# Key transposes one projection block earlier, and eight products in place of 32 behind the key products

## The chip, the cores and the metric

The kernel runs on one core of a Trainium2 chip. The metric is the device time of one execution in microseconds, the median of several. Nothing of the computation runs on the host, which only lays the arrays out.

## The reference

Three layers work on 256 tokens of width 1024 (and on 256 context tokens in the first): a hybrid mixer (gated delta rule beside attention) with a feed-forward part, a convolution layer with another, and a third layer of three branches. All is float32. The change lies in the gated delta rule of the first layer. Cut to that:

```python
decay = exp(where(incl, gcum[:, None] - gcum[None, :], -inf))
kb = kc * bc                                   # keys times beta
lower = where(strict, kb @ kc.T * decay, 0.0)  # one matrix for each chunk, head and direction
sol = triangular_solve(lower + eye, rhs, unit_diagonal=True)
```

The keys `kc` come from a projection, a convolution of five taps over the tokens, silu and a normalisation to length one. The rule runs once forward and once backward over the tokens, for 4 heads of width 128.

## The kernel before

The program is written out by hand for each engine: TensorE (PE), VectorE (DVE), ScalarE (ACT), GpSimd (POOL) and SyncE, which issues the weight loads. Each engine works through its own list in the order of the code, and semaphores tie the lists together; no scheduler moves anything. PSUM has eight banks, each given out in turns: `wait_full` waits until TensorE has filled a bank, `freed` gives it back.

The first layer's projection has twelve blocks of 128 features, numbered 0 to 11 (0 to 3 keys, 4 to 7 values, 8 to 11 queries). Blocks 0 to 4 are multiplied from weights that are split in two parts, a high one that ScalarE rounds (`part_high`, L1704) and a low one that VectorE subtracts (`part_low`, L2259); TensorE takes both in L987. The later blocks are multiplied in full precision (L789). ScalarE moves each block out of PSUM (`features_evac`, L1653), VectorE convolves it (`conv5`, L2306 and L2310) and ScalarE applies silu (`conv_silu`, L1659).

When key blocks 0 to 3 are through silu, TensorE turns them to rows of tokens (`to_tok`, L743), ScalarE squares and copies them (L1675, L1676), VectorE sums the squares (L2318) and scales the rows to length one (`unit_rows`, L2332). TensorE turns the scaled keys back (`to_feat`, L743 again), ScalarE copies (`to_features`, L1683), and TensorE multiplies the keys with each other, four products of one bank each (`kk`, L1026), one for each of the four stretches of 128 tokens. TensorE does projection blocks 5 and 9 between `to_tok` and `to_feat`, block 10 ahead of `kk`, and 11, 8, 6 and 7 behind it.

Each bank of key products then gives two matrices, one for each direction, in `U_t`: products times beta times decay, L2349. Beta differs by row and head, so each matrix takes four instructions of 128x128, one a head: 32 in all. The decays were written by ScalarE long before (`decays`, L1667); for stretches 0 and 1 they stand in `decay`, for 2 and 3 in `U_t` itself.

VectorE then transposes 32x32 blocks (L2359) beside ScalarE, which copies the other direction's blocks (L1762) when all four `ut_ready` are there and it has moved block 8 out of PSUM. From both VectorE builds the inverse of 32x32 blocks: L2362, 31 steps of L2368 and L2369, then L2396 and L2397. TensorE's products L1137 need the last of these. The wide part of the delta rule, the attention and the modulation products (L772, whose weights are loaded at that time) follow. Meanwhile, from 82.7 us to 112.1 us, GpSimd rotates and scales the attention's queries and keys (L2830 to L2855).

Of the kernel before, what the change touches and what calls it, by code (L numbers as in the profile page):

```python
# [25 lines left out]
ALU = mybir.AluOpType  # L26
# [4 lines left out]
P = 128  # L31
D = 1024
# [5 lines left out]
NH = 4  # L38
# [144 lines left out]
USE = {}  # L183
# [167 lines left out]
def build(nc, w, w_mod1, cols_in, rows_in, consts_in, b_out_in, c_bd_in, glu_in, b_in, x_in, ctx_in, out):  # L351
    ctx = ExitStack()
    w = {**w, "mod1": w_mod1}
    with ctx:
# [22 lines left out]
        def bc_in(ap, n):  # L377

            return ap.unsqueeze(2).to_broadcast([ap.shape[0], ap.shape[1], n])
# [18 lines left out]
        arena, arena_r = sb_both("arena", 16384)  # L398
        tok_t = sb("tok", TT * (HYB_T - 512) + TT * CTX_T)
        z_t, z_r = sb_both("z", TT * 512)  # L400
        o_t, o_r = sb_both("o", 1024)
# [26 lines left out]
        def bank(use):  # L428
            b = use[0] if isinstance(use, tuple) else use
            return psum[:, 512 * b:512 * b + 512]  # L430
# [51 lines left out]

        a_hi = [view(x, at, 2, 2 * T) for x, at in ((ybuf_r, 0), (ybuf_r, D), (arena_r, 2 * D), (arena_r, 3 * D))]
        a_lo = [view(x, at, 2, 2 * T) for x, at in ((yT_r, 0), (yT_r, D), (rowbc_r, 0), (diag_r, 0))]
        part_hi = [arena_r[:, 6144:6144 + D], o_r[:, 0:D], arena_r[:, 14432:14432 + D]]
        cv = view(arena, 0, 12, 2, T)
        cin = view(arena, 8192, 12, 2, T + 4)
        zgate = view(z_t, 0, TT, 512)
# [14 lines left out]
        U_t = [arena[:, 6144 + 512 * n:6656 + 512 * n] for n in range(4)] + [nrm_t[:, 512 * n:512 * n + 512] for n in range(4)]  # L503
        U_of = [view(arena, 6144, 16, P), view(nrm_t, 0, 16, P)]
        decay = view(decay_t, 0, 4, 512)
# [24 lines left out]
        beta = beta_t.rearrange("p (s e) -> p s e", s=4)  # L530
# [59 lines left out]
        kq_tok, kq_scaled, ut_ready, blocks_copied = sem("kq_tok"), sem("kq_scaled"), sem("ut_ready"), sem("blocks_copied")  # L590
# [78 lines left out]
        def wait_read(eng, use):  # L669
            eng.wait_ge(bank_free[use[0]], use[1] + 1)  # L670
# [4 lines left out]
        def freed(ins, use):  # L675
            ins.then_inc(bank_free[use[0]], 1)
# [56 lines left out]
        def _(pe):  # L733
# [268 lines left out]
            def hyb_features(c, blocks):  # L1002
                wait_ring(CHUNK["hyb_f", c])
                for b in blocks:
                    use = USE["hyb_f"][b]
                    wait_free(pe, use)
                    width = 2 * T if b < 8 else T
                    filled(feature_block(use, slot(CHUNK["hyb_f", c])[:, (b % 3) * D:(b % 3 + 1) * D],
                                         lambda k: aT[:, k, 0:width]), use)
# [27 lines left out]
            use = USE["gates"]  # L1037
# [15 lines left out]
                seq, t = (n // 2, n % 2)  # L1053
                transposes(USE["to_tok"][n], [cv[:, hh, seq, t * P:(t + 1) * P] for hh in range(NH)])
            hyb_features(1, (5,))
            hyb_features(3, (9,))
            for n in range(4):
                pe.wait_ge(kq_scaled, n + 1)
                transposes(USE["to_feat"][n], [ktok[:, n, hh * P:(hh + 1) * P] for hh in range(NH)])
            hyb_features(3, (10,))  # L1060
            for n in range(4):
                wait_read(pe, USE["to_feat"][n])
            for st in range(4):
                use = USE["kk"][st]
                wait_free(pe, use)
                kk = lambda hh: feat(kT[:, st // 2], st, hh)
                filled(per_head(use, kk, kk), use)
            hyb_features(3, (11,))
            hyb_features(2, (8, 6, 7))
            hyb_tokens(0)  # L1070

# [59 lines left out]
            for d in range(2):  # L1131
                use = USE["p5"][d]
                wait_free(pe, use)
                x, xt = inverse_of(d)
                for m in range(16):
                    for src, dst in PAIRS[d]:
                        last = mm(bank(use)[rows_of_block(dst), BLK * m:BLK * (m + 1)],  # L1137
                                  U_of[d][rows_of_block(src), m, rows_of_block(dst)], x[rows_of_block(src), m, :],
                                  start=True, stop=True)
                filled(last, use)  # L1140
            pause("p5")
            for d in range(2):
                wait_read(pe, USE["p5"][d])
                use = USE["q5"][d]
                wait_free(pe, use)
                x, xt = inverse_of(d)
                for m in range(16):
                    p = blk_p[:, 16 * d + m, :]
                    for src, dst in PAIRS[d]:
                        mm(bank(use)[rows_of_block(src), BLK * m:BLK * (m + 1)], p[rows_of_block(dst)],  # L1150
                           xt[rows_of_block(dst), m, :], start=True, stop=True)
                    src, dst = PAIRS[d][d]
                    last = mm(bank(use)[rows_of_block(dst), BLK * m:BLK * (m + 1)], xt[rows_of_block(dst), m, :],
                              p[rows_of_block(dst)], start=True, stop=True)
# [6 lines left out]
            for half, use in enumerate(USE["p6"]):  # L1161
                wait_free(pe, use)
                for m in range(8 * half, 8 * half + 8):
                    for d in range(2):
                        last = mm(bank(use)[halves[1 - d], 64 * (m % 8):64 * (m % 8 + 1)], U_of[d][halves[d], m, halves[1 - d]],
                                  X2[halves[d], m, :], start=True, stop=True)
# [8 lines left out]
            for half, use in enumerate(USE["q6"]):  # L1175
                wait_read(pe, USE["p6"][half])
                wait_free(pe, use)
                for m in range(8 * half, 8 * half + 8):
                    for d in range(2):
                        last = mm(bank(use)[halves[d], 64 * (m % 8):64 * (m % 8 + 1)], blk_p2[halves[1 - d], m, :],  # L1180
                                  XT_m[halves[1 - d], 16 * d + m, halves[1 - d]], start=True, stop=True)
# [25 lines left out]
            for s in range(4):  # L1207
                for d in range(2):
                    st = ORDER[d][s]
                    if s:  # L1210
                        wait_read(pe, USE["ds", s - 1, d])
                        use = USE["ks", s, d]
# [7 lines left out]
                for d in range(2):  # L1220
                    st = ORDER[d][s]
# [4 lines left out]
                    use = USE["vn", s, d]  # L1226
# [3 lines left out]
                if s >= 2:  # L1230
                    for d in range(2):
                        st = ORDER[d][s]
                        use = USE["os", s, d]
# [4 lines left out]
                if s < 3:  # L1238
                    for d in range(2):
                        wait_read(pe, USE["vn", s, d])  # L1240
                        pe.wait_ge(ktail_ready, 2 * s + d + 1)
                        use = USE["ds", s, d]
# [5 lines left out]
                if s >= 2:  # L1248
                    for d in range(2):
                        wait_read(pe, USE["vn", s, d])  # L1250
                        use = USE["oi", s, d]
# [68 lines left out]
            for n, src in enumerate((cc, csq)):  # L1320
                use = USE["ln"][n]
                wait_free(pe, use)
                order = [*CONV_PE, *(k for k in range(KT) if k not in CONV_PE)] if n == 0 else range(KT)
                for i, k in enumerate(order):
# [4 lines left out]
                    last = mm(bank(use)[:, 0:T], ones, src[:, k, :], start=(i == 0), stop=(i == KT - 1))  # L1329
# [83 lines left out]
            for i in range(S5T):  # L1413
# [7 lines left out]
                if i == 10:  # L1421
                    pe.wait_ge(logf_ready, 1)
                    use = USE["cum"]
# [19 lines left out]
            for n in range(NPAIR + 2):  # L1443
                if n < NPAIR:
                    pair, t = n // 2, n % 2
                    use = USE["fa_s"][n]
# [3 lines left out]
                    for half in range(2):  # L1450
                        q = slice(64 * half, 64 * half + 64)
                        last = mm(fa_scores[:, half, 0:(t + 1) * P], q2T[q, pair, t * P:(t + 1) * P], k2T[q, pair, 0:(t + 1) * P],  # L1452
                                  start=True, stop=True)
                    filled(last, use)
                    next(filler, None)
                if n >= 3 and n % 2:
                    pair = (n - 3) // 2
                    use = USE["fa_o"][pair]
                    wait_read(pe, USE["fa_t"][2 * pair + 1])
                    wait_free(pe, use)  # L1460
                    for kb, t0 in ((0, 0), (1, P)):
                        for half in range(2):
                            q0, at = 64 * half, (2 * pair + half) * AHD
                            last = mm(bank(use)[q0:q0 + 64, t0:T], v2[:, kb, at:at + AHD], fa_pT[pair % 2][:, half, kb, t0:T],
                                      start=(kb == 0), stop=(kb == 1))
# [16 lines left out]
            for j in range(8):  # L1482
# [3 lines left out]
                at = (j % 2) * 12 * P  # L1486
                for part in range(2):
                    use = USE["branch"][2 * j + part]
                    wait_free(pe, use)
                    for br in ((0, 1), (2,))[part]:  # L1490
                        for k in range(4):
                            wat = at + (4 * br + k) * P
                            last = mm(bank(use)[:, (br % 2) * T:(br % 2 + 1) * T], slot(c)[:, wat:wat + P],  # L1493
                                      ys[br][:, k, :], start=(k == 0), stop=(k == 3))
# [8 lines left out]
        def _(act):  # L1503
            fn = nc.scalar.activation
            ch = Chain(act, act_c)
# [142 lines left out]
            def features_evac(blocks):  # L1648
                for b in blocks:
                    use = USE["hyb_f"][b]  # L1650
                    wait_full(act, use)
                    n = 2 if b < 8 else 1
                    freed(fn(cin[:, b, 0:n, 2:T + 2], bank(use)[:, 0:n * T].rearrange("p (s t) -> p s t", s=n), ACT.Copy), use)  # L1653
# [75 lines left out]
            use = USE["gates"]  # L1729
# [22 lines left out]
            to_tokens(range(4))  # L1752
            act.wait_ge(kq_ms, 1)
            fn(kq_ss[:, 0:16], kq_ss[:, 0:16], ACT.Sqrt).then_inc(kq_sd, 1)
            features_evac((5, 9))
            to_features(range(4))
            features_evac((10,))
            conv_silu(5, (4,))
            features_evac((11, 8))
            act.wait_ge(ut_ready, 4)  # L1760
# [75 lines left out]
            for b in range(4):  # L1836
                last = fn(XT_m[rows_of_block(b), 0:16, rows_of_block(b)], xt[rows_of_block(b)], ACT.Copy)
# [5 lines left out]
            use = USE["q5"][0]  # L1843
# [3 lines left out]
            for src, dst in PAIRS[0]:  # L1847
                last = fn(XT_m[rows_of_block(src), 0:16, rows_of_block(dst)], grid[rows_of_block(src)], ACT.Copy, scale=-1.0)
# [5 lines left out]
            use = USE["q5"][1]  # L1854
# [212 lines left out]
        def _(dve):  # L2067
# [188 lines left out]
            def part_low(n):  # L2256
                dve.wait_ge(hyb_hi, 4 + n + 1)
                width = HYB_PARTS[n][3]
                tt(part_of(n, ring_r), part_of(n, ring), part_hi[n % 3][:, 0:width].bitcast(F32), ALU.subtract).then_inc(hyb_lo, 1)  # L2259
# [42 lines left out]
            def conv5(blocks):  # L2302
                n = 2 if blocks[0] < 8 else 1
                for b in blocks:
                    wait_read(dve, USE["hyb_f"][b])
                    ch.mark(ts(cv[:, b, 0:n, :], cin[:, b, 0:n, 0:T], taps[:, b, 0:1], None, ALU.mult))  # L2306
                for k in range(1, CONV_A):
                    ch.sync()
                    for b in blocks:
                        last = stt(cv[:, b, 0:n, :], cin[:, b, 0:n, k:k + T], taps[:, b, k:k + 1], cv[:, b, 0:n, :], ALU.mult, ALU.add)  # L2310
                        if k < CONV_A - 1:
                            ch.mark(last)
                last.then_inc(conv_done, 1)
# [18 lines left out]
                    tt(quad(x), quad(x), bc_in(kq_r[:, 4 * n:4 * n + 4], P), ALU.mult).then_inc(kq_scaled, 1)  # L2332

            conv5((0,))
            part_low(10)
            for b in range(1, 5):
                conv5((b,))
            unit_sums(0, 4)
            unit_rows(0, 4, None)
            conv5((5,))  # L2340
            for st, use in enumerate(USE["kk"]):
                wait_full(dve, use)
                for d in range(2):
                    n = 4 * d + st
                    wait_read(dve, USE["decay"][n])
                    src = decay[:, 2 * d + st, :] if st < 2 else U_t[n]
                    for hh in range(NH):
                        at = slice(hh * P, (hh + 1) * P)
                        last = stt(U_t[n][:, at], bank(use)[:, at], beta[:, st, 4 * d + hh:4 * d + hh + 1], src[:, at], ALU.mult, ALU.mult)  # L2349
                        if (d, hh) == (0, NH - 1):  # L2350
                            last.then_inc(ut_ready, 1)
                        elif hh == NH - 1:
                            freed(last, use)


            for use in USE["kk"]:
# [686 lines left out]
```

## Time and profile before

| | us |
|---|---|
| time, median of 3 runs (1362.14 to 1367.49) | 1363.67 |
| the profiled execution | 1363.14 |
| its span | 1361.1 |
| TensorE busy | 1279.1 (94%) |
| VectorE busy | 869.8 (64%) |
| ScalarE busy | 509.7 (37%) |
| GpSimd busy | 124.5 (9%) |

The page counts an engine as busy while an instruction stands on it, also if that instruction waits inside for something that no semaphore shows. The stretch that the change touches lies between 97 and 185 us of the span. All times below are counted from the span's start.

### The profile page before, as it was taken

Reading aid. Unit: us, or ns where it says so; the run is one execution under the profiler, and the core shown is the slowest. Engines: PE = TensorE matmul, PEld = TensorE weight load, DVE = VectorE, ACT = ScalarE, POOL = GpSimd, SP = SyncE. Lnnn points to the kernel's source line nnn. Section 1 sums busy time; section 2 is a strip of 40 time slices with the busy share of each in tenths; the row PEclk is TensorE's granted clock in tenths of the full one; section 3 lists DMA queues with packets and bytes.
Section 4 is the critical chain, followed back from the end, with each engine's and each line's share of the span. In section 5 each row is a group of like instructions: output and inputs, shape, how many; then the busy total and the mean of one; then the engine's idle time right before and its main releaser. Section 6 shows DMA issues by size and latency. Waiting matters only on the chain. (4 is left out here: it accounts for less than half of the span.)

```text
span 1361.1 us, 18882 instructions
## 1 busy us (share of the span) xinstructions
PE 1279.1 (94%) x7158; PEld 988.9 (73%) x7158; DVE 869.8 (64%) x1498; ACT 509.7 (37%) x850; POOL 124.5 (9%) x165
## 2 busy tenths in 40 slices
PE   3899979988999998999899999899999999899997
PEld 1687646553888887884588888777878885688886
DVE  1448796543876665795677777399962342777776
ACT  2474256323433444014544444312223321544443
POOL 0043022000000002000000000245520000000000
PEclk9899979999999999998899999899999999899999
DMA  9222367884555542421455555125233233455551
GB/s 391 89 112 77 138 269 287 356 353 180 195 189 186 185 155 70 155 94 47 185 186 185 185 185 198 66 78 185 93 139 127 106 109 123 155 185 185 185 189 58
DMA packets 24946, 225.75 MB, mean 166 GB/s; under 512 B 2737, under 2 KB 2865, under 8 KB 4658
## 3 DMA queue, kind: packets, MB, share of 16 engines
q1 hardware_dynamic: 23328, 220.31, 43.9%
q10 hardware_dynamic: 1554, 4.56, 0.9%
q8 instruction: 44, 0.72, 0.2%
q14 instruction: 20, 0.16, 0.0%
HBM read 223.81 MB, written 1.05 MB: 165 GB/s over the span
## 5 line engine op out<-in xcount | busy, mean ns | idle before, releaser
L872 PE MATMUL psum<-aT_r,arena_r 128*128 128x512 f32 x920 | 327.4, 398 | 1.4 <-DVE arena_r L2191 1.4
L2191 DVE TENSOR_TENSOR arena_r<-ring,arena_r 128x1024 fp32r<-128x1024 f32 x193 | 226.0, 1221 | 112.4 <-ACT arena_r L1599 112.4
L789 PE MATMUL psum<-aT,ring 128*128 128x256 f32 (+1 forms) x1136 | 266.3, 392 | 1.5 <-DVE aT L2148 1.5
L873 PE MATMUL psum<-aT_r,arena_r 128*128 128x256 f32 x920 | 258.2, 281 | 0.0
L789 PEld LDWEIGHTS psum<-aT,ring 128*128 128x128 f32 x1136 | 214.8, 191 | 47.9 <-issue 20.6
L1599 ACT ACTIVATE arena_r<-ring 128x1024 fp32r<-128x1024 f32 x193 | 191.5, 1050 | 149.6 <-PE psum L913 132.4
L913 PE MATMUL psum<-arena_r 128*128 128x512 f32 x876 | 213.5, 392 | 0.0
L872 PEld LDWEIGHTS psum<-aT_r,arena_r 128*128 128x128 f32 x920 | 172.8, 188 | 43.7 <-issue 1.9
L913 PEld LDWEIGHTS psum<-arena_r 128*128 128x128 f32 x876 | 159.5, 188 | 34.8
L873 PEld LDWEIGHTS psum<-aT_r,arena_r 128*128 128x128 f32 x920 | 173.7, 189 | 2.6
L1611 ACT ACTIVATE nrm<-nrm 128x256 f32<-128x256 f32 x76 | 31.8, 418 | 170.8 <-DVE nrm L2205 170.8
L772 PE MATMUL psum<-ring,cond 128*32 128x384 f32 x512 | 55.1, 560 | 20.2 <-DMA consts<-in_consts 12.4
L2205 DVE TENSOR_REDUCE nrm<-psum 128x256 f32<-128x512 f32 x76 | 51.9, 683 | 4.2 <-PE psum L883 4.2
L2535 DVE SCALAR_TENSOR_TENSOR arena<-arena,cols 128x256 f32<-128x256 f32 x120 | 52.8, 482 | 1.9
L772 PEld LDWEIGHTS psum<-ring,cond 128*32 128x32 f32 x512 | 15.2, 120 | 48.6 <-issue 36.0
L756 PE MATMUL psum<-consts,nrm 128*128 128x128 f32 x96 | 20.0, 382 | 29.5 <-DVE nrm L2121 27.5
L2219 DVE TENSOR_TENSOR nrm<-nrm 128x256 f32<-128x256 f32 x76 | 32.4, 426 | 21.8 <-ACT nrm L1611 16.1
L2209 DVE TENSOR_REDUCE nrm<-psum 128x256 f32<-128x512 f32 x44 | 30.4, 691 | 20.8 <-PE psum L873 20.8
L756 PEld LDWEIGHTS psum<-consts,nrm 128*128 128x128 f32 x96 | 16.5, 199 | 33.8 <-DVE nrm L2121 30.2
L2310 DVE SCALAR_TENSOR_TENSOR arena<-arena,cols 128x512 f32<-128x512 f32 (+1 forms) x48 | 35.3, 763 | 1.1
L1987 ACT ACTIVATE arena<-psum,cols 128x256 f32<-128x256 f32 x24 | 11.4, 474 | 58.2 <-PE psum L789 58.2
L2227 DVE TENSOR_TENSOR arena_r<-nrm,arena_r 128x256 fp32r<-128x256 f32 x73 | 31.1, 425 | 2.5
(495 smaller groups left out, 1642.3 us busy)
## 6 DMA issues: line engine op xcount, KB each, us to landing
ring<-in_w_ffn SPq DMA_DIRECT2D x44, 1536.0 KB, 6.5
ring<-in_w_mod SPq DMA_DIRECT2D x32, 1536.0 KB, 8.7
ring<-in_w_ff SPq DMA_DIRECT2D x32, 1024.0 KB, 4.9
ring<-in_w_in_g SPq DMA_DIRECT2D x8, 1536.0 KB, 6.4
ring<-in_w_conf_i SPq DMA_DIRECT2D x8, 1024.0 KB, 4.8
ring<-in_w_hyb_f SPq DMA_DIRECT2D x4, 1536.0 KB, 6.6
ring<-in_w_in_a SPq DMA_DIRECT2D x4, 1536.0 KB, 6.4
ring<-in_w_in_b SPq DMA_DIRECT2D x4, 1536.0 KB, 6.3
```

The costliest lines, as they stand in the source:

```text
L756: last = nc.tensor.transpose(bank(use)[:, j * T + t * P:j * T + (t + 1) * P], src[:, t, k * P:(k + 1) * P], ident)
L772: last = mm(mod_acc[q:q + 32, :], cond[:, at:at + 32], slot(c)[:, k * MOD_C:(k + 1) * MOD_C], start=(m == m0 and k < 4), stop=(m == m1 - 1 ...
L789: last = mm(bank(use)[:, out_at:out_at + rhs(k).shape[1]], weights[:, k * P:(k + 1) * P], rhs(k), start=(k == 0), stop=(k == KT - 1))
L872: mm(bank(use).rearrange("p (a t) -> p a t", a=2), hi, x_both[:, :, k, :], start=(k == 0), stop=False)
L873: last = mm(bank(use)[:, T:2 * T], lo, x_hi[:, k, :], start=False, stop=(k == KT - 1))
L913: last = mm(Y[:, t, half * 512:half * 512 + 512], act_part, w_part[:, half * 512:half * 512 + 512], start=(isinstance(i, int) and j == 0 a ...
L1599: fn(out_hi[2] if last_out else w_hi[j % 2][:, at], slot(c)[:, at], ACT.Copy).then_inc(split_hi, 1)
L2191: tt(lo, slot(c)[:, at], hi.bitcast(F32), ALU.subtract).then_inc(split_ready, 1)
L2205: summed = v.reduce_sum(g_sum[:, j % 2, :], bank(gate).rearrange("p (a t) -> p t a", a=2), axis=AXX)
L2219: tt(h_tmp, sg[:, j % 2, :], u_sum if parts == 3 else sg[:, j % 2, :], ALU.mult).then_inc(h_step, 1)
L2310: last = stt(cv[:, b, 0:n, :], cin[:, b, 0:n, k:k + T], taps[:, b, k:k + 1], cv[:, b, 0:n, :], ALU.mult, ALU.add)
L2535: last = stt(cc[:, c, :], cu[:, c, k:k + T], dww[:, c, k:k + 1], cc[:, c, :], ALU.mult, ALU.add)
```

## The change

VectorE multiplies the decays by beta ahead of the key products: eight instructions of 128x512, placed behind the convolution of block 0 and ahead of `part_low(10)`. Behind the key products stand eight instructions of 128x512 (`U_t` times a PSUM bank) in place of 32. TensorE does projection block 9 behind the `to_feat` transposes and not ahead of them, and block 10 behind `kk` and not ahead of it; ScalarE's copies follow suit. One buffer of rounded weights (`part_hi[0]`) moves, since `U_t` is now written while it is in use.

```diff
-        part_hi = [arena_r[:, 6144:6144 + D], o_r[:, 0:D], arena_r[:, 14432:14432 + D]]
+        part_hi = [arena_r[:, 4096:4096 + D], o_r[:, 0:D], arena_r[:, 14432:14432 + D]]
...
             hyb_features(1, (5,))
-            hyb_features(3, (9,))
             for n in range(4):
                 pe.wait_ge(kq_scaled, n + 1)
                 transposes(USE["to_feat"][n], [ktok[:, n, hh * P:(hh + 1) * P] for hh in range(NH)])
-            hyb_features(3, (10,))
+            hyb_features(3, (9,))
             for n in range(4):
                 wait_read(pe, USE["to_feat"][n])
...
                 filled(per_head(use, kk, kk), use)
-            hyb_features(3, (11,))
+            hyb_features(3, (10, 11))
             hyb_features(2, (8, 6, 7))
             hyb_tokens(0)
...
-            features_evac((5, 9))
+            features_evac((5,))
             to_features(range(4))
-            features_evac((10,))
+            features_evac((9, 10))
             conv_silu(5, (4,))
             features_evac((11, 8))
             act.wait_ge(ut_ready, 4)
...
             conv5((0,))
+            for n in range(8):
+                d, st = n // 4, n % 4
+                wait_read(dve, USE["decay"][n])
+                src = decay[:, 2 * d + st, :] if st < 2 else U_t[n]
+                ch.mark(tt(quad(U_t[n]), quad(src), bc_in(beta[:, st, 4 * d:4 * d + 4], P), ALU.mult))
             part_low(10)
             for b in range(1, 5):
                 conv5((b,))
             unit_sums(0, 4)
             unit_rows(0, 4, None)
             conv5((5,))
+            ch.sync()
             for st, use in enumerate(USE["kk"]):
                 wait_full(dve, use)
-                for d in range(2):
-                    n = 4 * d + st
-                    wait_read(dve, USE["decay"][n])
-                    src = decay[:, 2 * d + st, :] if st < 2 else U_t[n]
-                    for hh in range(NH):
-                        at = slice(hh * P, (hh + 1) * P)
-                        last = stt(U_t[n][:, at], bank(use)[:, at], beta[:, st, 4 * d + hh:4 * d + hh + 1], src[:, at], ALU.mult, ALU.mult)
-                        if (d, hh) == (0, NH - 1):
-                            last.then_inc(ut_ready, 1)
-                        elif hh == NH - 1:
-                            freed(last, use)
+                tt(U_t[st], bank(use), U_t[st], ALU.mult).then_inc(ut_ready, 1)
+                freed(tt(U_t[4 + st], bank(use), U_t[4 + st], ALU.mult), use)
```

VectorE's list of the changed kernel behind the convolution of block 0 (L2305 and L2309; in the kernel before they are L2306 and L2310): L2338 are the new products, L2258 is `part_low(10)`.

```order
L2309 SCALAR_TENSOR_TENSOR arena<-arena,cols 128x512 x4
L2338 TENSOR_TENSOR arena<-decay,small 128x512 x2
L2338 TENSOR_TENSOR arena<-arena,small 128x512 x2
L2338 TENSOR_TENSOR nrm<-decay,small 128x512 x2
L2338 TENSOR_TENSOR nrm<-nrm,small 128x512 x2
L2258 TENSOR_TENSOR ring_r<-ring,o_r 128x1024
```

In the kernel before `part_low(10)` stands right behind the convolution; eight instructions have moved in between, all of them ahead of the convolutions of blocks 1 to 4.

TensorE's list of the kernel before, from the `to_tok` transposes (the first L743) to the attention's; L789 are blocks 5 (128x512), then 9, the `to_feat` transposes, 10, the key products (L1026), 11 with 8, then 6 with 7:

```order
L743 MATMUL psum<-consts,arena 128x128 x16
L789 MATMUL psum<-aT,ring 128x512 x8
L789 MATMUL psum<-aT,ring 128x256 x8
L743 MATMUL psum<-consts,arena 128x128 x16
L789 MATMUL psum<-aT,ring 128x256 x8
L1026 MATMUL psum<-arena 128x128 x16
L789 MATMUL psum<-aT,ring 128x256 x16
L789 MATMUL psum<-aT,ring 128x512 x16
```

The same place in the changed kernel:

```order
L743 MATMUL psum<-consts,arena 128x128 x16
L789 MATMUL psum<-aT,ring 128x512 x8
L743 MATMUL psum<-consts,arena 128x128 x16
L789 MATMUL psum<-aT,ring 128x256 x8
L1026 MATMUL psum<-arena 128x128 x16
L789 MATMUL psum<-aT,ring 128x256 x24
L789 MATMUL psum<-aT,ring 128x512 x16
```

The second transposes and the key products each stand one block of eight 128x256 products earlier; what TensorE has done by the end of block 8 is the same set of instructions in both.

## Rows read from the trace of the kernel before

**Rows 1.** Timeline of VectorE: start, length, line, shapes, count, idle before and releaser

```profile
95.14 1.93 DVE L2259 TENSOR_TENSOR ring_r<-ring,arena_r 128x1024 fp32r<-128x1024 f32 x1 [4.05 <-ACT arena_r L1704]
...
97.69 6.03 DVE L2310 SCALAR_TENSOR_TENSOR arena<-arena,cols 128x512 f32<-128x512 f32 x4
107.61 1.23 DVE L2259 TENSOR_TENSOR ring_r<-ring,o_r 128x1024 fp32r<-128x1024 f32 x1 [3.88 <-ACT o_r L1704]
108.75 1.79 DVE L2306 TENSOR_SCALAR arena<-arena,cols 128x512 f32<-128x512 f32 x1
...
114.79 0.48 DVE L2306 TENSOR_SCALAR arena<-arena,cols 128x512 f32<-128x512 f32 x1
...
118.86 3.12 DVE L2310 SCALAR_TENSOR_TENSOR arena<-arena,cols 128x512 f32<-128x512 f32 x4
```

**Rows 2.** Timeline of GpSimd beside it

```profile
94.44 1.54 POOL L2843 TENSOR_TENSOR ring<-ring,rows 128x640 f32<-128x640 f32 x1
...
97.34 1.71 POOL L2843 TENSOR_TENSOR ring<-ring,rows 128x640 f32<-128x640 f32 x1
...
99.99 1.90 POOL L2848 TENSOR_TENSOR ring<-ring,consts 128x640 f32<-128x640 f32 x1
101.86 2.61 POOL L2851 TENSOR_TENSOR ring<-ring,consts 128x320 f32<-128x320 f32 x2
104.43 1.57 POOL L2848 TENSOR_TENSOR ring<-ring,consts 128x640 f32<-128x640 f32 x1
105.96 1.71 POOL L2851 TENSOR_TENSOR ring<-ring,consts 128x320 f32<-128x320 f32 x2
107.74 4.23 POOL L2855 TENSOR_TENSOR ring<-ring 128x640 f32<-128x640 f32 x2
```

**Rows 3.** Timeline of TensorE from the last product of block 4

```profile
122.09 0.39 PE L987 MATMUL psum<-arena_r,ring_r 128*128 128x512 f32 x1
122.69 1.53 PE L743 MATMUL psum<-consts,arena 128*128 128x128 f32 x12 [0.22 <-ACT arena L1659]
...
140.64 2.84 PE L1026 MATMUL psum<-arena 128*128 128x128 f32 x24
143.95 1.16 PE L1026 MATMUL psum<-arena 128*128 128x128 f32 x8 [0.47 <-DVE nrm L2349]
```

**Rows 4.** Timeline of ScalarE

```profile
122.01 0.63 ACT L1659 ACTIVATE arena<-arena 128x512 f32<-128x512 f32 x1 [2.92 <-DVE arena L2310]
...
152.05 0.39 ACT L1653 ACTIVATE arena<-psum 128x256 f32<-128x256 f32 x1 [3.07 <-PE psum L789]
152.33 2.57 ACT L1762 ACTIVATE yT<-arena 32x512 f32<-32x512 f32 x4
```

**Rows 5.** Timeline of VectorE from the scaled keys on

```profile
130.08 2.50 DVE L2332 TENSOR_TENSOR arena<-arena 128x512 f32<-128x512 f32 x4
...
141.73 1.12 DVE L2349 SCALAR_TENSOR_TENSOR arena<-psum,small,decay 128x128 f32<-128x128 f32 x4 [5.38 <-PE psum L1026]
...
150.23 2.90 DVE L2359 STREAM_TRANSPOSE yT<-nrm 32x512 f32<-32x512 f32 x4
...
155.00 2.09 DVE L2362 STREAM_TRANSPOSE diag<-yT 128x1024 f32<-128x1024 f32 x1 [1.87 <-ACT yT L1762]
```

**Rows 6.** Timeline of TensorE, its three waits that the clock is read beside

```profile
184.46 1.10 PE L1137 MATMUL psum<-yT,arena 32*32 32x32 f32 x58 [2.08 <-DVE yT L2397]
...
533.22 3.40 PE L756 MATMUL psum<-consts,nrm 128*128 128x128 f32 x16 [4.33 <-DVE nrm L2121]
...
862.98 3.67 PE L756 MATMUL psum<-consts,nrm 128*128 128x128 f32 x16 [4.25 <-DVE nrm L2121]
```

**Rows 7.** Windows: busy us by engine, then granted TensorE clock, DMA share, GB/s

```profile
186.00:188.00 2.00, 2.00 (x54) 1.48 (x53) 1.97 (x3) 1.87 (x4) 1.88 (x3) 0.50 0.98 418
...
534.00:536.00 2.00, 2.00 (x11) 1.72 (x10) 1.58 (x5) 0.14 (x1) 0.96 (x4) 0.50 0.00 0
...
868.00:870.00 2.00, 2.00 (x6) 1.64 (x5) 0.00 (x0) 0.00 (x0) 1.84 (x4) 0.50 0.00 0
```

## The prediction

> **What bounds the kernel now.** I read the page first (TensorE has work on it for 94% of the span), then the timelines of each engine from 95 to 185 us, then the waits there. I follow back what the changed stretch hands on. TensorE's products L1137 at 184.46 waited 2.08 us for VectorE's L2397 [rows 6]; that is the end of VectorE's inversion, which runs without a gap from L2362 at 155.00 on. L2362 itself sat idle for 1.87 us until ScalarE's copies L1762 had ended, although VectorE's own work of the key products was done by 153.13 (150.23 + 2.90) [rows 5]. L1762 came right behind ScalarE's move of block 8 at 152.05, for which ScalarE had waited 3.07 us on TensorE [rows 4]. So the chain is: TensorE's list up to the end of block 8, ScalarE's move and copies, VectorE's inversion, TensorE again. VectorE's 32 products L2349 are not on it: they end before L2362 could start, with 1.87 us to spare.
>
> TensorE's list up to block 8 has few gaps. Two matter. Ahead of the `to_tok` transposes it waits 0.22 us for silu of block 3, and inside the key products 0.47 us for a bank that L2349 held [rows 3]. Silu of block 3 starts at 122.01 [rows 4], right when VectorE's convolution of block 3 ends (118.86 + 3.12 = 121.98) [rows 1]. VectorE therefore has no slack at 122 us: it and TensorE arrive together. Its one free time before is the 3.88 us ahead of `part_low(10)` at 107.61 [rows 1].
>
> **The change part by part.**
>
> *Eight products in place of 32.* Before, VectorE takes 8.5 us from 141.73 to 150.23. After, eight products of 128x512; the nearest row is L2332, 2.50 us for four, 0.625 each, so about 5.0 us. With `kk` one block earlier they would end near 143.5 and the transposes near 146.5. Saved on VectorE's list: some 6 us. On the chain: nothing, since L2362 still waits for ScalarE's copies, which wait for block 8. What is late next is the same thing as now. The one gain is the 0.47 us of TensorE's bank wait: a bank is now freed 1.3 us after it is filled, and three further fills of 0.9 us come first.
>
> *The reordered blocks.* Up to the end of block 8 TensorE does the same instructions. The scaled keys come at 130.7 to 132.6 (four of L2332 from 130.08) and `to_feat` would start at 131.9, so the earlier transposes wait for at most a tenth or two. Block 9's weights are there already, block 10's bank too. Cost and gain: nothing.
>
> *The eight products ahead.* They are 8 x 0.625 = 5.0 us of VectorE's time, put ahead of `part_low(10)`, where 3.88 us are free. Were this all, `part_low(10)` would start at 103.72 + 5.0 = 108.7 instead of 107.61. But GpSimd is at work there until 111.97 [rows 2], and the rows show what that does. The TENSOR_SCALAR at 108.75 took 1.79 us against 0.48 at 114.79, while an L2855 ran, and the four SCALAR_TENSOR_TENSOR at 97.69 took 6.03 us against 3.12 at 118.86 [rows 1]. The TENSOR_TENSOR at 95.14, the kind that is added, took 1.93 us against 1.23 for the same shape at 107.61, under L2843 [rows 1, 2]. GpSimd's own two L2855 stretched as well. VectorE and GpSimd take turns there, an instruction at a time.
>
> From 103.72 on GpSimd still has 0.75 us of L2851, 1.57, 1.71, and two L2855 (4.23 us less the some 1.4 that they stood blocked): 6.9 us of its own work. How much of it VectorE loses has two bounds. The four instructions at 97.69 lost 2.9 us while GpSimd went through L2843, L2848, one L2851 and a small one between, about 4 us by their shorter rows (1.54, 1.57, 0.86) [rows 2]: 0.7 of it, which is 4.8 us here. Block 1's convolution, 108.75 to 114.79, took 6.04 us; blocks 2 and 3 together, 114.79 to 121.98, took 7.19, or 3.6 each [rows 1]. The two L2855 thus took 2.4 us from VectorE for 2.8 of their own, 0.9 of it: 6.2 us here. I take 5.2, nearer the first, as L2848 and L2851 are the same instructions. Block 1's convolution does not lose its 2.4 us again: it now comes after GpSimd is done.
>
> So VectorE: 103.72 + 5.0 (products) + 1.14 (`part_low`) + 5.2 (turns lost) = 115.1. TensorE needs `part_low(10)` for block 4, whose 24 products of 0.23 us begin about 5.5 us ahead of 122.3 [rows 3], at 116.8: 1.7 us of cover are left, and with the upper bound 0.7. Then three convolutions, 3 x 3.6 = 10.8: block 3 ends at 125.9 in place of 121.98. That is 3.9 us late (3.5 to 4.9), and nothing hides it: silu, `to_tok` and, in ScalarE's list, the move of block 4 and all of the key chain are behind it, and TensorE's list stands.
>
> **The sum.** +3.9 at `to_tok`, -0.5 at `kk`, all else moves along (the loads behind these blocks too, as they wait for their slots): +3.4 us. The profiled execution would go from 1363.14 to 1366.5; it lies 0.5 us under the median, so 1363.67 + 3.4 = 1367.1. A difference of under 0.5% (6.8 us) is about what a measurement of this kernel cannot tell from none.
>
> The Trainium skill ("SBUF — State Buffer", section Who interferes with whom) says that a VectorE instruction with two SBUF inputs and a GpSimd instruction that reads SBUF exclude each other for the whole instruction. By that rule alone, with no overlap at the handovers, the loss would be the full 6.9 us and the total +5.1; the rows show 0.7 to 0.9 of it, so I go by them.
>
> **The rivals.**
>
> *TensorE's clock falls in the new gap, for short.* TensorE would sit idle from 122.5 to about 126.6, 4.1 us. After idle times of 4.33 and 4.25 us the granted clock read 0.50, the lower of its two levels, and after 2.08 us with light work around it too [rows 6, 7]. Against it: dense work comes right before and behind. At half clock half of the time is lost: some 3.4 us low costs 1.7, total +5.1, 1368.8. Chance 25%.
>
> *The same, for long: slower by over 0.5%.* From 862 to 870 us the clock stayed low [rows 7]. The change is slower by over 0.5% if the clock is low for more than (6.8 - 3.4) / 0.5 = 6.8 us of work in blocks 5, 9 and the key products. With 10 us it would be +8.4, 1372.1. For it: that row. Against it: there work was thin until 867, here it is not. Chance 13%.
>
> *The products ahead are hidden.* If the new form, whose second input is a small broadcast, is not held up by GpSimd, `part_low(10)` ends at 109.9, block 1's convolution meets only the last L2855 (1.2 us lost), the three end at about 121.9, and only the 0.5 us at `kk` remains: 1363.2. For it: no row shows this form beside GpSimd. Against it: three other kinds are held up. Chance 14%.
>
> *The drain of the key products sets the end after all: faster.* If L2362 could start with VectorE's own work done, at 146.5 and not 155.0, the gain would be 8.5 less the 3.9 of delay: -4.6, 1359.1; with the products hidden too, -8.5. It needs ScalarE's copies ahead of block 8, and their order in its list says otherwise. Chance 4%. The last 4% are for what I don't see.
>
> **How the numbers follow.** The main case has 40%; its own range is +3.0 to +4.4, so 1366.7 to 1368.1. The range must take in the hidden case's neighbourhood below in part and the short clock fall above, and the spread of medians of some 1 us: 1362.7 to 1371.0 leaves about 18% out. Faster by over 0.5% needs the last rival with both its parts, 2%, or 1% of what I don't see: 3%. Slower by over 0.5% is the long clock fall and again 1% of what I don't see: 14%. The rest is within 0.5%.
>
> **What would show it.** Right: L2338 with a mean well over 0.7 us while GpSimd runs, `part_low(10)` ending near 115, the convolution of block 3 near 125.9, TensorE idle for some 4 us ahead of `to_tok`, no bank wait inside `kk`, VectorE idle for 8 us or so ahead of L2358 (L2362 before), still released by ScalarE's copies, and these by block 8. Wrong: L2338 at 0.63 us each, or L2358 released by VectorE's own transposes. The clock row of 122 to 134 us tells the first two rivals from the main case.

## The result, and the profile after

| | before | changed |
|---|---|---|
| median of 15 runs, us | 1363.77 | 1369.94 |
| the profiled execution | 1363.14 | 1370.66 |
| its span | 1361.1 | 1368.6 |

The ratio is 1.0044, 95% interval 1.0036 to 1.0052: 6.2 us slower, more than the forecast 3.4. It is under the 0.5% that I had drawn as the line, but the interval tells it clearly from none. One of the 15 executions before, at 1876.55 us, does not count in the ratio. The profiled execution of the changed kernel lies 0.7 us over its median. In its trace everything at 95 us is already 0.2 us later than in that of before, which I take off where I say so.

VectorE's timeline of the changed kernel. L2338 are the eight products ahead; L2309, L2258 and L2305 answer to L2310, L2259 and L2306 of [rows 1]:

```profile
103.90 3.34 DVE L2338 TENSOR_TENSOR arena<-decay,small 128x512 f32<-128x512 f32 x2
107.16 2.65 DVE L2338 TENSOR_TENSOR arena<-arena,small 128x512 f32<-128x512 f32 x2
109.73 4.02 DVE L2338 TENSOR_TENSOR nrm<-decay,small 128x512 f32<-128x512 f32 x2
113.68 1.28 DVE L2338 TENSOR_TENSOR nrm<-nrm,small 128x512 f32<-128x512 f32 x2
114.88 1.21 DVE L2258 TENSOR_TENSOR ring_r<-ring,o_r 128x1024 fp32r<-128x1024 f32 x1
...
123.11 0.90 DVE L2305 TENSOR_SCALAR arena<-arena,cols 128x512 f32<-128x512 f32 x1
124.04 3.11 DVE L2309 SCALAR_TENSOR_TENSOR arena<-arena,cols 128x512 f32<-128x512 f32 x4
```

GpSimd's timeline beside it:

```profile
102.10 2.61 POOL L2847 TENSOR_TENSOR ring<-ring,consts 128x320 f32<-128x320 f32 x2
104.67 2.02 POOL L2844 TENSOR_TENSOR ring<-ring,consts 128x640 f32<-128x640 f32 x1
106.65 2.61 POOL L2847 TENSOR_TENSOR ring<-ring,consts 128x320 f32<-128x320 f32 x2
109.34 3.86 POOL L2851 TENSOR_TENSOR ring<-ring 128x640 f32<-128x640 f32 x2
...
122.77 0.95 POOL L2856 MEMSET arena<- 128x1024 f32 x1 [9.41 <-PE psum L987]
```

The last two products, when GpSimd is done, take 1.28 us together (0.68 each, one beginning a little ahead of the other's end), the six before them 1.36 or 2.05 each. The line's own answer, in short windows, shows the three lengths (count, ns min/median/max, start):

```profile
L2338 DVE TENSOR_TENSOR arena<-decay,small x1: 1365/1365/1365, 103.9 to 103.9; 128x512 f32<-128x512 f32 x1
L2338 DVE TENSOR_TENSOR arena<-decay,small x1: 2057/2057/2057, 105.2 to 105.2; 128x512 f32<-128x512 f32 x1
L2338 DVE TENSOR_TENSOR nrm<-nrm,small x1: 676/676/676, 113.7 to 113.7; 128x512 f32<-128x512 f32 x1
```

One GpSimd instruction lets one VectorE instruction through: a product takes 1.36 us beside a 128x320, 2.05 beside a 128x640, 0.68 alone. The record of each counts the wait as busy time. The convolution of block 3 ends at 127.15 (124.04 + 3.11), against 121.98 before.

TensorE's timeline, which answers to [rows 3]:

```profile
122.32 0.39 PE L987 MATMUL psum<-arena_r,ring_r 128*128 128x512 f32 x1
127.87 3.68 PE L743 MATMUL psum<-consts,arena 128*128 128x128 f32 x16 [5.16 <-ACT arena L1658]
131.34 7.13 PE L789 MATMUL psum<-aT,ring 128*128 128x512 f32 x16
138.31 2.06 PE L743 MATMUL psum<-consts,arena 128*128 128x128 f32 x16
140.21 3.62 PE L789 MATMUL psum<-aT,ring 128*128 128x256 f32 x16
143.66 3.73 PE L1026 MATMUL psum<-arena 128*128 128x128 f32 x32
```

The wait ahead of the first transposes is 5.16 us in place of 0.22, and the bank wait inside the key products is gone. The windows around it (busy us of PE, PEld, DVE, ACT and POOL, then the granted clock) show that TensorE's clock went to its lower level in that wait and stayed there under the transposes:

```profile
122.00:124.00 2.00, 0.71 (x4) 0.25 (x2) 1.96 (x3) 0.63 (x1) 1.17 (x2) 1.00 0.00 0
124.00:126.00 2.00, 0.00 (x0) 0.00 (x0) 1.89 (x4) 0.00 (x0) 0.20 (x2) 0.68 0.00 0
126.00:128.00 2.00, 0.13 (x1) 0.13 (x2) 1.12 (x2) 0.81 (x2) 0.00 (x0) 0.50 0.00 0
128.00:130.00 2.00, 2.00 (x10) 2.00 (x11) 1.59 (x3) 1.28 (x4) 0.00 (x0) 0.50 0.00 0
130.00:132.00 2.00, 2.00 (x10) 1.76 (x9) 1.93 (x4) 2.00 (x6) 0.00 (x0) 0.61 0.00 0
132.00:134.00 2.00, 2.00 (x6) 0.82 (x5) 2.00 (x4) 1.98 (x4) 0.00 (x0) 1.00 0.00 0
```

ScalarE's timeline, which answers to [rows 4]:

```profile
157.80 0.38 ACT L1652 ACTIVATE arena<-psum 128x256 f32<-128x256 f32 x1 [3.07 <-PE psum L789]
158.08 2.56 ACT L1761 ACTIVATE yT<-arena 32x512 f32<-32x512 f32 x4
```

VectorE's, which answers to [rows 5]:

```profile
149.02 0.68 DVE L2349 TENSOR_TENSOR nrm<-psum,nrm 128x512 f32<-128x512 f32 x1
149.83 2.90 DVE L2355 STREAM_TRANSPOSE yT<-nrm 32x512 f32<-32x512 f32 x4
160.75 2.10 DVE L2358 STREAM_TRANSPOSE diag<-yT 128x1024 f32<-128x1024 f32 x1 [8.01 <-ACT yT L1761]
```

The drain of the key products, up to the start of the 32x32 transposes, went from 8.5 us to 5.0 (144.82 to 149.83), and VectorE now waits 8.0 us ahead of the inversion in place of 1.9. The chain through block 8 and ScalarE's copies is the same; it is 5.75 us later, 5.5 with the 0.2 taken off.

### The profile page after: what moved, and what is told of

Its sections match the earlier page's. It is cut to its first block and busy times, and to the rows that moved or that the text cites. A ratio compares the mean times of both kernels' runs of the same rounds, so it can differ in the third digit from the quotient of the medians.

```text
span 1368.6 us, 18862 instructions
## 1 busy us (share of the span) xinstructions
PE 1278.7 (93%) x7158; PEld 989.6 (72%) x7158; DVE 876.2 (64%) x1482; ACT 509.4 (37%) x850; POOL 125.2 (9%) x165
## 5 line engine op out<-in xcount | busy, mean ns | idle before, releaser
L789 PE MATMUL psum<-aT,ring 128*128 128x256 f32 (+1 forms) x1136 | 267.9, 394 | 1.5 <-DVE aT L2147 1.5
L789 PEld LDWEIGHTS psum<-aT,ring 128*128 128x128 f32 x1136 | 216.1, 193 | 47.9 <-issue 20.1
L2309 DVE SCALAR_TENSOR_TENSOR arena<-arena,cols 128x512 f32<-128x512 f32 (+1 forms) x48 | 34.1, 739 | 1.1
```

Source lines behind the costliest of these rows:

```text
L789: last = mm(bank(use)[:, out_at:out_at + rhs(k).shape[1]], weights[:, k * P:(k + 1) * P], rhs(k), start=(k == 0), stop=(k == KT - 1))
```

## The experiments

My theory: the loss comes from the eight products ahead, which take turns with GpSimd and push the convolutions, and so TensorE, back. Its rivals: the new order of blocks costs; five more us of VectorE's work cost wherever they stand; the clock takes a part. Ratios are to the kernel before, run on the same chip; their 95% intervals stand in brackets. Each trace is of one execution, and where that lies far from the median of its kernel I say so.

**e1: the order alone.** The diff shows TensorE's part; ScalarE's copies follow suit.

```diff
             hyb_features(1, (5,))
-            hyb_features(3, (9,))
...
-            hyb_features(3, (10,))
+            hyb_features(3, (9,))
...
-            hyb_features(3, (11,))
+            hyb_features(3, (10, 11))
```

> The kernel before with the new order of TensorE's blocks 9 to 11 and of ScalarE's copies alone; the 32 products stay behind the key products. If the loss comes from the products ahead (my theory): the key products start near 137.2 us, 3.4 earlier, VectorE waits longer ahead of L2362, still for ScalarE's copies behind block 8, and the time is that of before, between -0.8 and +0.5 us. If the new order is what costs: most of the +6.2 us.

Measured: 1364.51, ratio 0.9999 (0.9991 to 1.0008). The key products (L1026) start at 137.67, VectorE waits 5.3 us ahead of the inversion for the same copies. The order costs nothing and gives nothing that 11 executions can tell (within some 1.2 us).

```profile
137.67 2.84 PE L1026 MATMUL psum<-arena 128*128 128x128 f32 x24
140.98 1.16 PE L1026 MATMUL psum<-arena 128*128 128x128 f32 x8 [0.47 <-DVE nrm L2348]
```

**e2: the products alone.** The changed kernel with the order of before, in TensorE and in ScalarE; the eight products ahead and the eight behind stay.

> The changed kernel with TensorE's and ScalarE's order of before: only the products ahead and the eight behind are left. My theory: VectorE loses 6 us to GpSimd, TensorE waits 5 us ahead of the first transposes, +5.5 to +6.5 us against before. If the new order costs: near 0.

Measured: 1370.51, ratio 1.0050 (1.0036 to 1.0065). The wait ahead of the transposes is 5.16 us here too. All of the loss is in the products.

**e3: the products late.** e2 with the loop of eight moved:

```diff
             conv5((0,))
-            for n in range(8):
-                ...
             part_low(10)
...
             conv5((5,))
+            for n in range(8):
+                ...
             ch.sync()
```

> As e2, but the eight products by beta stand behind the convolution of block 5, right ahead of the key products, where VectorE is idle for 5.4 us before and GpSimd does nothing. My theory: each takes 0.62 us, no wait ahead of the first transposes, between -0.8 and +0.3 us against before. If five more us of VectorE's work cost wherever they stand: +3 us or more.

Measured: 1363.41, ratio 1.0000 (0.9989 to 1.0010). The same eight products, in VectorE's timeline:

```profile
136.53 1.29 DVE L2345 TENSOR_TENSOR arena<-decay,small 128x512 f32<-128x512 f32 x2
137.73 1.29 DVE L2345 TENSOR_TENSOR arena<-arena,small 128x512 f32<-128x512 f32 x2
```

They take 4.9 us, VectorE is back 0.6 us before the first key products, and the loss is gone. It is the place that costs. This kernel also has the moved buffer `part_hi[0]`, so that move costs nothing either.

**e4: TensorE's gap filled.** VectorE as in the changed kernel; TensorE and ScalarE take block 5 ahead of the first transposes, 9 and 10 ahead of the second. The diff shows TensorE's part.

```diff
+            hyb_features(1, (5,))
             pe.wait_ge(silu_done, 4)
...
-            hyb_features(1, (5,))
+            hyb_features(3, (9, 10))
             for n in range(4):
                 pe.wait_ge(kq_scaled, n + 1)
...
-            hyb_features(3, (9,))
...
-            hyb_features(3, (10, 11))
+            hyb_features(3, (11,))
```

> The changed kernel with projection block 5 ahead of the first transposes and blocks 9 and 10 ahead of the second: TensorE has 6.9 us of work where it waited 5.2. VectorE still loses its turns. My theory: no wait of over 1 us ahead of either transposes, the granted clock stays at its upper level from 122 to 150 us, a wait of some 1.5 us inside the key products since VectorE's block 5 now comes late; +0.5 to +2 us against before. If the key chain on VectorE were what sets the end: no better than +5 us.

Measured: 1363.98, ratio 1.0000 (0.9990 to 1.0010), a little better than expected. VectorE loses the same turns (3.34, 2.65, 4.02 us for the first three pairs), yet TensorE runs from 122.17 on with one wait of 0.35 and one of 0.95 us up to the key products, and the inversion starts at 154.50 (in an execution 2.1 us over the median). So VectorE's delay costs nothing as long as TensorE has other work meanwhile.

**e6: GpSimd's rest left out.** The changed kernel without L2847's four instructions and L2851's two, so that the attention's queries and keys are turned wrongly.

```diff
-                for c in range(2):
+                for c in range(0):
                     s4 = sin_t[:, t, :].rearrange("p (b c d) -> p b c d", b=2, c=2)[:, :, c, :]
...
-            for t in range(TT):
-                ch.mark(tt(rot_a[:, t, :], rot_a[:, t, :], rot_b[:, t, :], ALU.add))
```

> The changed kernel with six of GpSimd's instructions left out (the sine half of the rotation and its sum, so the attention's queries and keys are turned wrongly): GpSimd is then done by about 104 us, and the products ahead run alone. My theory: they take 0.65 us each in place of 1.4, block 3's convolution ends by 122, no wait of over 1 us ahead of the first transposes; between -0.8 and +0.8 us against before. If their own 5 us were the cause and not the turns: +3 us or more.

Measured: 1364.53, ratio 1.0000 (0.9990 to 1.0010). VectorE's timeline (this kernel's profiled execution is its slowest, 3.0 us over the median):

```profile
104.96 1.28 DVE L2338 TENSOR_TENSOR arena<-decay,small 128x512 f32<-128x512 f32 x2
...
108.57 1.28 DVE L2338 TENSOR_TENSOR nrm<-nrm,small 128x512 f32<-128x512 f32 x2
109.77 1.21 DVE L2258 TENSOR_TENSOR ring_r<-ring,o_r 128x1024 fp32r<-128x1024 f32 x1
```

At the same place in the list, with nothing beside them, the eight products take 4.8 us (104.96 to 109.77), TensorE has no wait ahead of the first transposes, and the loss is gone.

**e5: the control.** The same edit in the kernel before.

> Control: the kernel before with the same six instructions of GpSimd left out. My theory: block 1's convolution takes 3.6 us in place of 6.0, the 0.2 us wait ahead of the first transposes goes or stays, nothing else depends on it: between -0.8 and +0.4 us against before. If leaving them out itself made the kernel faster by more than that, the run of the changed kernel without them would prove less.

Measured: 1365.46, ratio 1.0014 (1.0006 to 1.0023). It did not come out as expected: 1.9 us slower by the ratio, though nothing up to the inversion moved (L2362 at 155.07). Its profiled execution lies another 1.9 us over its median, so the trace can't well say where the difference arises, and its cause is open. For e6 it means that leaving the work out does not by itself make the kernel faster; with that work out of both, the kernel with the products ahead (e6) is no slower than the one without them.

**e9 and e10: the gap kept warm.** Small products that nobody reads, put in TensorE's gap of the changed kernel so that the clock does not fall; 40 in e9, 20 in e10.

```diff
             features_in_parts((1, 2, 3, 4))
+            pe.wait_ge(mod_taken, 1)
+            for n in range(40):
+                mm(mod_out, ident, ident, start=True, stop=True)
```

> The changed kernel with 40 small products of the identity with itself, whose result nobody reads, where TensorE waited 5.2 us ahead of the first transposes: they end before silu does, so nothing starts later. If 1 to 2 us of the loss come from the clock that falls in that wait: the granted clock stays at its upper level, the sixteen transposes take 2.2 us in place of 3.7, and the time is 0.7 to 2 us under that of the changed kernel, +4.2 to +5.5 against before. If the clock costs nothing: as the changed kernel, +6 us.

Measured: 1372.99, ratio 1.0063 (1.0050 to 1.0077). I had sized it wrongly: the 40 took 8.9 us, not the 4.5 that I meant, and the transposes began 2.9 us later than in the changed kernel (130.73). The inversion began only 1.6 us later (162.31).

> As e9 with 20 products: each turned out to take 0.22 us, so 20 take 4.5 and end before silu does. If the fallen clock is part of the loss (the trace of e9 says about 1.3 us): the first transposes start 5.2 us late as in the changed kernel, at the upper level of the clock, and VectorE's inversion (L2358 of the changed kernel) starts 1 to 1.5 us sooner than its 160.8; +4.3 to +5.4 us against before. If the clock costs nothing: inversion at 160.8, +6 us.

Measured: 1369.62, ratio 1.0043 (1.0030 to 1.0056). The clock reads 1.00 in every window from 120 to 132 us; two of them, from an execution 1.3 us over the median:

```profile
128.00:130.00 2.00, 1.58 (x13) 1.34 (x13) 1.34 (x3) 1.74 (x5) 0.00 (x0) 1.00 0.00 0
130.00:132.00 2.00, 2.00 (x8) 1.21 (x9) 1.93 (x3) 2.00 (x5) 0.00 (x0) 1.00 0.00 0
```

The inversion starts 1.0 us sooner:

```profile
128.12 1.53 PE L743 MATMUL psum<-consts,arena 128*128 128x128 f32 x12 [0.69 <-ACT arena L1661]
...
159.75 2.10 DVE L2361 STREAM_TRANSPOSE diag<-yT 128x1024 f32<-128x1024 f32 x1 [8.01 <-ACT yT L1764]
```

From the first transposes to the inversion it is 31.6 us here and in e9, and 32.9 in the changed kernel: the fallen clock costs 1.25 us in that stretch. In the whole time the gain does not show, against the +4.3 to +5.4 that I expected; but the ratio's interval spans 3.5 us, and six executions can't tell 1.25 us. So the clock's part is shown at its place, and not in the total.

**e7, e8, e11, e12: what the saved time is worth.** e7 is the kernel before with ScalarE's copies moved ahead; e8 is e3 with the same edit.

```diff
-            features_evac((11, 8))
             act.wait_ge(ut_ready, 4)
             for b in range(4):
                 fn(blk_c[rows_of_block(b), 0:16, :], U_of[0][rows_of_block(b), :, rows_of_block(b)], ACT.Copy).then_inc(blocks_copied, 1)
+            features_evac((11, 8))
```

> The kernel before with one edit: ScalarE's four copies stand ahead of its moves of blocks 11 and 8. If, as I read it, block 8 sets the start of the inversion: it is then set by the 32 products and their transposes, L2362 starts at 153.2 in place of 155.0, and the time falls by 1 to 2 us. If the copies were not what it waits for: nothing.

Measured: 1363.02, ratio 0.9999 (0.9990 to 1.0007). The inversion starts at 153.27, released by VectorE's own transposes, so the copies were what it waited for. The time does not follow, where I had expected 1 to 2 us: TensorE's L1137 starts 1.7 us sooner, at 182.80, and the first L820, behind the delta rule, at 301.2 against 301.0. L1150 now stands idle for 5.7 us in place of 4.2 for nothing that the profile shows, and TensorE's waits for modulation weights between 150 and 310 us come to 6.3 us in place of 4.8.

> e3 (eight products late, order of before) with e7's edit. The inversion can start when VectorE's transposes end, near 150.0, and ends near 180; TensorE still has filler products of the modulation until 182.4 and so gains only the 2.1 us that it waited: -1.5 to -2.5 us against before, hardly more than e7. If eight for 32 is worth what VectorE saves: -4 us or more.

Measured: 1362.56, ratio 0.9990 (0.9980 to 1.0000), 1.4 us by the ratio and so just under the forecast 1.5 to 2.5: inversion at 149.18, L1137 at 181.16, first L820 at 299.1.

e11 is e8 with one filler product of the modulation behind L1137:

```diff
-    "qk": "MSMM", "p5": "M", ...
+    "qk": "MSM", "p5": "MM", ...
```

> e8 with one of TensorE's modulation products (1.5 us, behind a wait of 0.7 for its weights) moved from ahead of L1137 to behind it: L1137 can start near 180.5 in place of 184.5. If the saved time of VectorE is real once nothing hides it: -2.5 to -4.5 us against before and under e8. If weights or the later chain take it back: as e8.

Measured: 1360.72, ratio 0.9979 (0.9969 to 0.9989), the only kernel whose whole interval lies under 1; L1137 starts at 178.54, 5.9 us sooner than before, and first L820 at 296.8, 4.2 sooner. The profiled execution is the fastest of the twelve, 2.2 us under the median, so its trace flatters the kernel; by the ratio 2.9 us, about half of the 5.9, arrive in the time.

e12 is the kernel before, with its 32 operations behind the key products and its order of blocks, and the two edits above: the copies ahead and the filler product behind L1137.

> e7 (the 32 products of before, ScalarE's copies ahead) with e11's moved modulation product. It tells what of e11's gain is due to eight products in place of 32: the inversion starts near 153.2 in place of 148.9, L1137 near 182.7 in place of 180.9. If the form of the products is worth something once nothing hides it: 1 to 2.5 us slower than e11, -0.5 to -2 us against before. If moving the filler is all that counts: as e11, -2.9 us.

Measured: 1363.56, ratio 0.9992 (0.9981 to 1.0003). With the 32 products the inversion starts at 152.82 and TensorE waits for its end again:

```profile
182.25 1.30 PE L1137 MATMUL psum<-yT,arena 32*32 32x32 f32 x58 [2.38 <-DVE yT L2397]
```

So eight products in place of 32 may be worth some 1.8 us (0.9992 against 0.9979), on condition that they stand late, that the copies don't wait for block 8, and that the filler doesn't cover it. The traces show the 3.7 us at L1137 (178.54 against 182.25); the 1.8 in the time is not shown, since the two ratios were taken on different chips and their intervals overlap.

## Why the prediction was right, and where its size was off

*What sets the end.* Right: the inversion waited for ScalarE's copies and they for block 8, before and after. e1 took 3 us off the drain's end for nothing.

*The drain.* Right: 8.5 us became 5.0, as forecast, and is worth nothing here. Its one gain, the bank wait of 0.47 us, came as forecast.

*The turns with GpSimd.* The mechanism was right, the term too small. I put the lost turns at 5.2 us between bounds of 4.8 and 6.2; from 103.90 to 114.88 eight products took 11.0 us against the 4.8 that they take alone in e6, so 6.2 were lost. That it falls on my upper bound is luck: 2.4 of 2.8 is 0.86, which I had rounded up to 0.9, and unrounded the bound is 5.9. My lower bound came from L2310 of before, and single instructions show why it does not carry over:

```profile
L2310 DVE SCALAR_TENSOR_TENSOR arena<-arena,cols x3: 829/1904/1941, 97.7 to 100.5; 128x512 f32<-128x512 f32 x3
L2310 DVE SCALAR_TENSOR_TENSOR arena<-arena,cols x2: 1251/1596/1941, 100.5 to 102.5; 128x512 f32<-128x512 f32 x2
L2310 DVE SCALAR_TENSOR_TENSOR arena<-arena,cols x2: 752/752/752, 112.6 to 113.3; 128x512 f32<-128x512 f32 x2
```

Alone an L2310 takes 0.75 us (the last row). Beside a GpSimd instruction of 128x640 it became 1.2 us longer (1.90 and 1.94), a product 1.4; beside one of 128x320 it became 0.5 longer (1.25), a product 0.7. And one of the four, beside the end of a GpSimd instruction of 128x128, lost almost nothing (0.83). Why the two kinds lose differently is open.

*The convolutions behind.* 3.6 us each, right, but for one thing that I left out: block 3's TENSOR_SCALAR, now beside GpSimd's memset at 122.77, took 0.90 us in place of 0.48. Block 3 ended at 127.15, not 125.9, 4.95 us late with the shift taken off, not 3.9: past the 3.5 to 4.9 that I had given.

*TensorE's clock.* I had it as a rival, at 25%, with 1.7 us. It fell, and cost 1.25. The forecast of 1367.1 was the case without it, and that case's own range, 1366.7 to 1368.1, misses the 1369.94; the case with it, 1368.8, is nearer to what happened. The wide range holds the result because it took in this rival.

The sum with measured terms: +4.95 at the first transposes, +1.25 clock, -0.47 bank wait make +5.7 at the inversion, where the trace has +5.5. At L1137 (L1136 in the changed kernel) it is still 5.5 (190.21 against 184.46, less the 0.2). The medians differ by 6.2; the other 0.7 us lie within the interval of the ratio (4.9 to 7.1 us).

What the Trainium skill says ("SBUF — State Buffer", Who interferes with whom), that such instructions exclude each other whole, would have had 6.9 us of turns lost; 6.2 were, against my 5.2. The runs here agree with it, but for that 0.7 over six handovers, for the product with a broadcast second input, which no row of before had shown beside GpSimd (0.68 us alone, 1.36 and 2.05 beside it).

Open: why the stretch from L1137 to the first L820 took between 116.5 us (before) and 119.9 (e10) in kernels that do the same work there. Most of it seems to be one execution against another and not one kernel against another: where the profiled execution lies within 0.7 us of its kernel's median or under it (before, changed, e1, e2, e3, e9) the stretch took 116.5 to 117.4 us, and where it lies 1.3 to 3.0 over it (e4, e5, e6, e10) 118.7 to 119.9. With one trace of each kernel this is not shown, and what differs inside the stretch is open.

## What to carry to other kernels

Before moving work into an engine's idle time, look at what its neighbour does in that time: VectorE's 3.9 free us lay beside GpSimd's work, and 5 us of products became 11. Then ask what the moved work stands ahead of; here it stood ahead of the convolutions for which TensorE waited, and a place 33 us later cost nothing. A shorter drain is worth something only if nothing later releases the next step: read the releaser of the wait behind it first.

## What the runs showed of the hardware

A float32 product of 128x128 took 0.22 us in e9, as two records; I had read the 0.11 us of one record as the whole product. A GpSimd memset, which reads nothing, held up a TENSOR_SCALAR of VectorE by 0.42 us (0.90 against 0.48), while the SCALAR_TENSOR_TENSOR with two SBUF inputs that ended beside its start was not lengthened (2.33 for the three at 120.86, 0.78 each). The kernel before shows it too, at block 4: its memset ran from 122.54 to 123.49, and the TENSOR_SCALAR from 123.16 took 0.61 us. Both ended 0.28 or 0.29 us behind the end of their memset.
